# A two-layer encoder: the first two units behind each inner norm multiply x times gain, and the root and shift enter afterwards

## The chip, the core and the metric

The kernel runs on one core of a Trainium2 chip. The time is device microseconds of one execution from launch to end; a verdict compares medians of runs on the same chip. TensorE does the products, VectorE and ScalarE the elementwise work, POOL (GpSimd) and SP mostly issue loads.

## The reference, cut to what matters

Two sequences, 256 and 512 rows of 1024 features, go through two layers. Each layer normalizes, mixes, adds, normalizes again and applies a gated feed-forward:

```
def rmsnorm(x, g):  y = x * rsqrt(mean(x*x) + EPS);  return y * g
def modulate(h, shift, scale): return h * (1 + scale) + shift
h = modulate(rmsnorm(x, norm1_g), sh1, sc1);  x = x + g1 * mixer(h)
h = modulate(rmsnorm(x, norm2_g), sh2, sc2);  x = x + g2 * ((silu(h @ Wg) * (h @ Wu)) @ Wdown)
```

With r the reciprocal root of a row, w = g * (1 + scale) and s the shift, h = (x * w) * r + s. So h @ W = ((x * w) @ W) * r + s @ W: the root scales the result of a row, and the shift adds one vector per sequence. After the second layer a last norm gives the output. The mixer is attention and gated linear attention in layer 0 (even) and an mLSTM in layer 1 (odd).

## The kernel before, in words

All of x is kept turned: 8 tiles of 128 features (partitions) by 768 columns, 256 of the first sequence and 512 of the second. A product keeps fp32 precision by splitting both operands in two (hi and lo, float32r) and adding hi*hi, hi*lo and lo*hi: three products, each of 256 and 512 moving columns. A **feature unit** is 128 output features, k = 8 such triples for the projections from h (6 or 8 for the down projections, 4 for outb0 and outa0). A **token unit** is 256 output features with h as the stationary operand. plan_units (L69) lists the units in their order: bqk0, lowrank0, bv0, aq0, ak0, bg0, av0, outb0, outa0; then three groups gu00, down00, gu01, down01, gu02, down02; the odd layer's cq1, gates1, ck1, cv1 and co1, out1, then gu10 to down12. The gu units alternate gate (even n) and up (odd n).

Each engine has its own queue, written out in that order; semaphores tie them. Weights lie in four slots: SP's load of a unit waits for the products of the unit four before it (L594); ScalarE makes w_hi (split_to, L1213, L1221), VectorE w_lo (L1588, L1601), each one or two units ahead, in front of the work for the current unit. A feature unit's result lies in a pair of PSUM banks (L271); u.pair (L402) turns over three pairs in gu and down units and over two elsewhere, and a unit waits (wait_free, L738) until the former user of its pair has been read.

**Norms.** n = 0 is the one at the start, 1 stands behind outa0, 2 behind down02, 3 behind out1, 4 at the end. While the eight units before a norm give the last parts of x (residual, L1727; x is updated at L1737, 256 and then 512 columns), ScalarE squares each tile (squares_of and square_tile, L1274 to L1287) and VectorE sums the squares (add_squares, L1662). TensorE then adds over features with products of one column (norm_sums: L773 for the sum of seven, L776 for the last square), VectorE and ScalarE make mean, root and reciprocal (mean_root, L1669; ScalarE's norm, L1289), VectorE writes the root into six diagonal matrices (L1683), and TensorE spreads them over all partitions into bank pair 2 (L785). Then h is made tile by tile in VectorE's norm (L1678) and ScalarE's norm: normed = x * w * r (scaled, L1688), h_hi = normed + shift (L1297), h_lo = (normed + shift) - h_hi (rest, L1695), with two buffers of normed. The order on VectorE is scaled(0), scaled(1), rest(0), scaled(2), rest(1) and so on. TensorE runs the first two units behind the norm together (two_feature_tiles, L831), product k of both as soon as h of tile k is there, and then single units (feature_tile, L814).

A gu pair is taken so (hidden, L1312 and L1745): ScalarE makes silu of the gate unit into silu_g (L1322), VectorE prod = silu_g * up (L1757), ScalarE act_hi (L1326), VectorE act_lo (L1760). In gu00 to down01 VectorE also computes the modulation of the later norms (modulate, L1604; lines L1617 and L1620) from loads that POOL issues (L709), and TensorE sums it (L765). Those parts stand in VectorE's queue in front of the take of their unit (run, L1640).

## Time and profile before

| | us |
|---|---|
| median of 3 runs | 2128.09 (2118.55 to 2129.23) |
| profiled execution, its own time | 2124.51 |
| its span, first to last instruction | 2122.4 |
| TensorE busy with products | 2017.7 |
| VectorE busy | 992.6 |
| ScalarE busy | 601.7 |
| mean granted TensorE clock | 0.967 of full |

Some 2.1 us of the profiled execution's time lie around its span. Busy times are sums over the span; a granted clock of 1.00 is 2.4 GHz, 0.50 is 1.2 GHz. A time in a timeline is counted from the span's start.

### The profile page before, as it was taken

How to read it: one execution, taken by the hardware profiler on the slowest of the kernel's cores; microseconds unless marked ns; L12 is line 12 of the kernel's file. 1: busy time of each engine (PE TensorE's matmuls, PEld its weight loads, DVE VectorE, ACT ScalarE, POOL GpSimd, SP SyncE). 2: the span in 40 equal slices, each digit the busy share in tenths (PEclk: the TensorE clock that was granted, in tenths of full speed). 3: DMA queues.
4: the chain of work that ended last, by engine and by line, in shares of the span. 5: the costliest groups of instructions: out<-in, count | busy, mean ns of one | idle time of the engine just before them, and what ended most of it. 6: DMA issues, size and time to landing. Idle time of an engine off the chain costs nothing.

```text
span 2122.4 us, 28746 instructions
## 1 busy us (share of the span) xinstructions
PE 2017.7 (95%) x12081; PEld 1742.5 (82%) x12081; DVE 992.6 (47%) x1875; ACT 601.7 (28%) x1101; POOL 74.3 (4%) x121
## 2 busy tenths in 40 slices
PE   7879999988899999999998999998989999999998
PEld 2768888767788888888887788888878888888887
DVE  1877425684766665652235334544452222222224
ACT  3235224652321112211223333334232211211213
POOL 2010000000011101100000000000000000000000
PEclk9889999999899999999998999999989999999999
DMA  7343112012344444432223201021212222222212
GB/s 282 120 150 108 41 41 80 21 31 60 99 142 138 136 122 139 142 96 60 65 62 104 60 20 41 21 99 49 61 50 60 60 70 60 64 66 60 62 56 82
DMA packets 210249, 174.16 MB, mean 82 GB/s; under 512 B 10320, under 2 KB 196792, under 8 KB 208584
## 3 DMA queue, kind: packets, MB, share of 16 engines
q1 hardware_dynamic: 197536, 117.67, 18.5%
q0 software_dynamic: 12288, 48.35, 7.1%
q10 hardware_dynamic: 296, 6.29, 0.7%
q8 instruction: 96, 1.57, 0.3%
q14 instruction: 33, 0.27, 0.0%
HBM read 162.85 MB, written 9.44 MB: 81 GB/s over the span
## 4 chain that ended last, share of the span: by engine, by line
PE 87%; DVE 6%; ACT 4%; issue 2%; DMA 1%; POOL 0%; ACTq 0%; DVEq 0%; POOLq 0%
PE bank L824 60%; PE bank L790 9%; PE bank L842 4%; PE bank L1096 2%; PE bank L747 1%; PE bank L765 1%; DMA early_raw<-in_w_mod_dram 1%; ACT w_hi L1221 1%; DVE early_acc L1620 1%; DVE w_lo L1601 1%; PE bank L1018 1%; PE bank L908 1%; PE bank L1041 1%; PE bank L966 1%; PE bank L1068 1%
## 5 line engine op out<-in xcount | busy, mean ns | idle before, releaser
L824 PE MATMUL bank<-h_hi,w_hi 128*128 128x256 f32 x1600 | 409.4, 338 | 0.1
L824 PE MATMUL bank<-h_lo,w_hi 128*128 128x256 f32 x1600 | 407.5, 336 | 0.0
L824 PE MATMUL bank<-h_hi,w_lo 128*128 128x256 f32 x1600 | 407.3, 336 | 0.0
L1601 DVE TENSOR_TENSOR w_lo<-raw,w_hi 128x1024 fp32r<-128x1024 f32 (+4 forms) x195 | 239.0, 1230 | 340.2 <-ACT w_hi L1221 340.1
L824 PEld LDWEIGHTS bank<-h_hi,w_lo 128*128 128x128 f32 x1600 | 301.3, 188 | 33.6
L824 PEld LDWEIGHTS bank<-h_lo,w_hi 128*128 128x128 f32 x1600 | 301.4, 188 | 33.2
L824 PEld LDWEIGHTS bank<-h_hi,w_hi 128*128 128x128 f32 x1600 | 299.4, 188 | 34.2 <-issue 1.9
L1221 ACT ACTIVATE w_hi<-raw 128x1024 fp32r<-128x1024 f32 (+4 forms) x196 | 205.6, 1053 | 226.3 <-DMA raw<-in_ffn_w_down_dram 129.1
L790 PE MATMUL bank<-w_hi,h_hi 128*128 128x256 f32 x672 | 214.8, 320 | 18.1 <-DVE w_lo L1601 17.7
L790 PE MATMUL bank<-w_lo,h_hi 128*128 128x256 f32 x672 | 195.8, 291 | 0.0
L790 PE MATMUL bank<-w_hi,h_lo 128*128 128x256 f32 x672 | 195.6, 291 | 0.0
L1737 DVE SCALAR_TENSOR_TENSOR x<-bank,mod,x 128x256 f32<-128x256 f32 (+1 forms) x144 | 82.3, 613 | 229.6 <-PE bank L824 225.6
L824 PE MATMUL bank<-act_hi,w_hi 128*128 128x256 f32 x704 | 179.4, 337 | 4.6 <-issue 4.6
L824 PE MATMUL bank<-act_lo,w_hi 128*128 128x256 f32 x704 | 178.8, 336 | 0.0
L824 PE MATMUL bank<-act_hi,w_lo 128*128 128x256 f32 x704 | 178.7, 336 | 0.0
L790 PEld LDWEIGHTS bank<-w_hi,h_hi 128*128 128x128 f32 x672 | 134.5, 200 | 31.0 <-DVE w_lo L1601 18.1
L824 PEld LDWEIGHTS bank<-act_hi,w_hi 128*128 128x128 f32 x704 | 131.7, 188 | 19.8 <-issue 5.8
L824 PEld LDWEIGHTS bank<-act_lo,w_hi 128*128 128x128 f32 x704 | 132.4, 188 | 14.5
L824 PEld LDWEIGHTS bank<-act_hi,w_lo 128*128 128x128 f32 x704 | 132.4, 188 | 14.4
L790 PEld LDWEIGHTS bank<-w_lo,h_hi 128*128 128x128 f32 x672 | 134.6, 200 | 4.9 <-issue 3.8
L790 PEld LDWEIGHTS bank<-w_hi,h_lo 128*128 128x128 f32 x672 | 134.4, 200 | 0.0
L1620 DVE SCALAR_TENSOR_TENSOR late_acc<-late_raw,c_cols,late_acc 128x512 f32<-128x512 f32 x196 | 133.7, 746 | 0.6 <-DMA late_raw<-in_w_mod_dram 0.6
(274 smaller groups left out, 2251.7 us busy)
## 6 DMA issues: line engine op xcount, KB each, us to landing
raw<-in_ffn_w_gu_dram SPq DMA_DIRECT2D x176, 256.0 KB, 3.3
late_raw<-in_w_mod_dram POOLq DMA_DIRECT2D x56, 512.0 KB, 4.3
raw<-in_ffn_w_down_dram SPq DMA_DIRECT2D x64, 256.0 KB, 3.3
early_raw<-in_w_mod_dram POOLq DMA_DIRECT2D x24, 512.0 KB, 4.4
wide<-in_w_mod_dram SPq DMA_DIRECT2D x8, 1024.0 KB, 18.7
raw<-in_odd_w_in_dram SPq DMA_DIRECT2D x16, 512.0 KB, 4.4
raw<-in_even_w_in_dram SPq DMA_DIRECT2D x24, 256.0 KB, 5.0
x_kept<-x ACTq DMA_DIRECT2D x2, 3072.0 KB, 10.3
```

The costliest lines, as they stand in the source:

```text
L747: last = mm(bank[4 + c][0:2, :], c_cols[:, k, :], wide[k][:, c * 512:(c + 1) * 512], start=(k == 0), stop=(k == KD - 1))
L765: last = mm(mod_column(l, c0 // P + m)[:, s:s + 1], mod_acc(b)[:, s, m * P:(m + 1) * P], ones[:, 0:1], start=True, stop=True)
L790: last = mm(out, stationary[a], moving[b], start=(k == 0 and n == 0), stop=(k == K - 1 and n == 2))
L824: last = mm(pair(u.pair)[s], wk[a], seq(operand(o, k), s), start=(k == 0 and n == 0), stop=(k == u.ks - 1 and n == 2))
L842: last = mm(pair(u.pair)[s], wk[a], seq(operand(o, k), s), start=(k == 0 and n == 0), stop=(k == u.ks - 1 and n == 2))
L908: last = transpose(out[s][:, c:c + P], source(t), ident[:])
L966: last = mm(bank[6][:, d * P:(d + 1) * P], k_e[c][rows, t * P:(t + 1) * P], q_e[c][rows, t * P:(t + 1) * P], start=True, stop=True)
L1096: last = mm(bank[7][:, 0:C_V + 1], weights[d][:, c:c + P], z_cv[:, h, i, :], start=(i == froms[0]), stop=(i == froms[-1]))
L1221: fn(hi, r, ACT.Copy).then_inc(hi_ready, 1)
L1601: v.tensor_tensor(lo, r, hi.bitcast(F32), ALU.subtract).then_inc(unit_split, 1)
L1620: ins = v.scalar_tensor_tensor(acc, mod_raw(m)[:, kk, :], c, acc, ALU.mult, ALU.add)
L1737: last = v.scalar_tensor_tensor(seq(x[:, f, :], s), pair(u.pair)[s], mod[l][:, gate + f, s:s + 1], seq(x[:, f, :], s), ALU.mult, ALU.add)
```

## The change

The rows of h get two columns in front (hs_hi, hs_lo: 770 columns instead of 768), for the shift of the two sequences; a row so begins 8 bytes later in a step of 3080 bytes instead of 3072. All users of h read the rows at their new place.

At norms 1, 2 and 3 every residual unit is followed by plain (VectorE: normed = x * w, then h_lo = normed - h_hi) with ScalarE's copy into h_hi between. The first of them also writes the shift into the two columns. TensorE runs the first two units on these plain rows (two_plain_tiles); the first sequence's product has 258 moving columns, so that shift @ W comes out as two more result columns. The mean products stand behind k = 1 and the row products behind k = 3 of these two units. norm_sums is cut into norm_means and norm_rows for that, with no other change. ScalarE copies the spread root from bank pair 2 to SBUF (rstd_wide); scaled reads it there. After its fifth normed VectorE takes the first unit (take_first: the two shift columns, then result * root), after its sixth h_hi ScalarE applies shift and Identity or Silu (first_shifted); the second unit is taken at its usual place. h with root and shift is then made as before, over the plain rows, and serves from the third unit on, which waits for each of its tiles. VectorE and ScalarE split the weights of the third and fourth unit inside the norm. The cq units turn over three bank pairs.

The diff, without the declaration of the new semaphores and the cutting of norm_sums, with its indentation reduced:

```diff
@@ -134,9 +134,10 @@
-H = region(2 * KD * ROW)
-h_hi = at("h_hi", H, [P, KD, T], F32R)
-h_lo = at("h_lo", H + KD * ROW, [P, KD, T], F32R)
+H = region(2 * KD * (ROW + 8))
+hs_hi = at("hs_hi", H, [P, KD, 2 + T], F32R)
+hs_lo = at("hs_lo", H + KD * (ROW + 8), [P, KD, 2 + T], F32R)
+h_hi, h_lo = hs_hi[:, :, 2:2 + T], hs_lo[:, :, 2:2 + T]
@@ -150,6 +151,8 @@
 normed = [at(f"normed{b}", Z + 76 * KB + b * ROW, [P, T]) for b in range(2)]
+rstd_wide = at("rstd_wide", Z + 82 * KB, [P, T])
+first_bias = at("first_bias", Z + 85 * KB, [P, 2, 2])
@@ -271,6 +274,15 @@
     return bank[2 * g][:, 0:256], bank[2 * g + 1][:, 0:512]
+def wide_pair(g):
+    return bank[2 * g][:, 0:258], bank[2 * g + 1][:, 0:512]
+def wide_seq(ap, s):
+    return ap[:, 0:258] if s == 0 else ap[:, 258:770]
+NORM_AT = {1: (0, 1), 2: (1, 0), 3: (1, 1)}
@@ -399,7 +419,7 @@
         by = "act"
-    pairs = 3 if base in ("gu", "down") else 2
+    pairs = 3 if base in ("gu", "down", "cq") else 2
@@ -424,6 +444,7 @@
+MEANS_AFTER, ROWS_AFTER = 1, 3
@@ -473,6 +494,12 @@
     splittable.setdefault(-1 if u.prior is None else u.prior, []).append(u)
+def first_units(n):
+    return phase[{1: "gu00", 2: "cq1", 3: "gu10"}[n]][:2]
+FIRST_SCALED = {1: 1, 2: 2, 3: 4}
@@ -845,6 +879,29 @@
+    def two_plain_tiles(us, n):
+        for u in us:
+            pe.wait_ge(unit_split, u.i + 1)
+            wait_free(u)
+        pe.wait_ge(shift_ready, n)
+        for k in range(KD):
+            pe.wait_ge(plain_ready, KD * (n - 1) + k + 1)
+            for u in us:
+                wk = [slot_of(wt, u)[:, k * P:(k + 1) * P] for wt in (w_hi, w_lo)]
+                for m, (a, o) in enumerate(((0, 0), (0, 1), (1, 0))):
+                    for s in range(2):
+                        last = mm(wide_pair(u.pair)[s], wk[a], wide_seq((hs_hi, hs_lo)[o][:, k, :], s),
+                                  start=(k == 0 and m == 0), stop=(k == KD - 1 and m == 2))
+                if k == KD - 1:
+                    last.then_inc(group_full, 1)
+            if k < KD - 1:
+                last.then_inc(plain_read, 1)
+            if k == MEANS_AFTER:
+                norm_means(n)
+            if k == ROWS_AFTER:
+                norm_rows(n)
@@ -855,8 +912,19 @@
-    def feature_units(name, before=None, operand=normal, mix=None):
+    def feature_units(name, before=None, operand=normal, mix=None, norm=None):
         us = phase[name]
+        if norm:
+            two_plain_tiles(us[:2], norm)
+            after(us[0])
+            after(us[1])
+            pe.wait_ge(rstd_taken, norm)
+            feature_tile(us[2], operand, after_norm(norm), mix)
+            after(us[2])
+            for u in us[3:]:
+                feature_tile(u, operand, None, mix)
+                after(u)
+            return
@@ -1166,20 +1234,17 @@
     feature_units("outa0", lambda k: pe.wait_ge(mix_lo, B_HEADS + k + 1), turned(0), mix)
-    norm_sums(1)
     for g in range(FG):
-        feature_units(f"gu0{g}", after_norm(1) if g == 0 else None)
+        feature_units(f"gu0{g}", norm=1 if g == 0 else None)
         down_units(0, g)
-    norm_sums(2)
     mix = mix_odd()
-    feature_units("cq1", after_norm(2))
+    feature_units("cq1", norm=2)
...
     feature_units("out1", lambda k: pe.wait_ge(mix_lo, KD + k + 1), turned_odd, mix)
-    norm_sums(3)
     for g in range(FG):
-        feature_units(f"gu1{g}", after_norm(3) if g == 0 else None)
+        feature_units(f"gu1{g}", norm=3 if g == 0 else None)
@@ -1249,6 +1314,10 @@
         def take(u):
+            if u.name == "cq1" and u.n < 2:
+                if u.n == 1:
+                    first_shifted(2, u)
+                return
@@ -1282,21 +1351,52 @@
                 fn(dummy[:], ones[:, 0:1], ACT.Sqrt)
+            if n in NORM_AT and u.n == 0:
+                l, i = NORM_AT[n]
+                act.wait_ge(mod_ready, 7 if l == 0 else 1 + len(MOD_BLOCKS))
+                fn(hs_hi[:, :, 0:2], mod[l][:, (SH1, SH2)[i]:(SH1, SH2)[i] + KD, :], ACT.Copy).then_inc(shift_hi, 1)
...
             square_tile(n, u.n)
+            if n in NORM_AT:
+                act.wait_ge(plain_scaled, KD * (n - 1) + u.n + 1)
+                fn(h_hi[:, u.n, :], normed[u.n % 2][:], ACT.Copy).then_inc(plain_hi, 1)
...
+    def first_shifted(n, u):
+        act.wait_ge(first_scaled, FIRST_SCALED[n] + u.n)
+        dest, f = (z_o[:, 2 * u.n, :], ACT.Identity) if n == 2 else (silu_g[:], ACT.Silu)
+        for s in range(2):
+            last = fn(seq(dest, s), seq(dest, s), f, bias=first_bias[:, u.n, s:s + 1])
+        last.then_inc(free_act if n == 2 else silu_ready, 1)
     def norm(n, i):
+        if n in NORM_AT:
+            split_to(first_units(n)[0].i - 2)
...
         fn(mean_sq[:], mean_sq[:], ACT.Sqrt).then_inc(root_ready, 1)
+        if n in NORM_AT:
+            split_to(first_units(n)[0].i - 1)
...
             return
+        if n in NORM_AT:
+            act.wait_ge(rstd_full, TILES * (n + 1))
+            for s in range(2):
+                last = fn(seq(rstd_wide, s), pair(2)[s], ACT.Copy)
+            last.then_inc(rstd_taken, 1)
...
             act.wait_ge(normed_ready, KD * n + f + 1)
+            if n in NORM_AT:
+                if f < KD - 1:
+                    act.wait_ge(plain_read, (KD - 1) * (n - 1) + f + 1)
+                else:
+                    act.wait_ge(group_full, first_units(n)[1].g1)
...
             last.then_inc(h_hi_ready, 1)
+            if n in NORM_AT and f == 5:
+                first_shifted(n, first_units(n)[0])
@@ -1314,6 +1414,8 @@
             j = u.n // 2
+            if g == 0 and u.n == 0:
+                return
@@ -1681,12 +1783,19 @@
             v.tensor_scalar(rstd_diag[:, t, :], ident[:], mean_sq[:, t:t + 1], None, ALU.mult).then_inc(rdiag_ready, 1)
+        if n in NORM_AT:
+            split_to(first_units(n)[0].i - 1)
         dve.wait_ge(rstd_full, TILES * (n + 1))
+        rows = pair(2)
+        if n in NORM_AT:
+            dve.wait_ge(rstd_taken, n)
+            rows = seq(rstd_wide, 0), seq(rstd_wide, 1)
...
                 m = v.scalar_tensor_tensor(seq(normed[f % 2], s), seq(x[:, f, :], s), gain[l][i][:, f, s:s + 1],
-                                           pair(2)[s], ALU.mult, ALU.mult)
+                                           rows[s], ALU.mult, ALU.mult)
@@ -1703,6 +1812,8 @@
                 rest(f - 1)
+            if n in NORM_AT and f == 4:
+                take_first(n, first_units(n)[0])
@@ -1723,6 +1834,49 @@
         m.then_inc(mix_lo, 1)
+    def plain(n, f, u):
+        l, i = NORM_AT[n]
+        if f == 0:
+            dve.wait_ge(shift_hi, n)
+            v.tensor_tensor(hs_lo[:, :, 0:2], mod[l][:, (SH1, SH2)[i]:(SH1, SH2)[i] + KD, :],
+                            hs_hi[:, :, 0:2].bitcast(F32), ALU.subtract).then_inc(shift_ready, 1)
+        dve.wait_ge(free_dve, u.free[0][1])
+        if f >= 2:
+            dve.wait_ge(plain_ready, KD * (n - 1) + f - 1)
+        for s in range(2):
+            last = v.tensor_scalar(seq(normed[f % 2], s), seq(x[:, f, :], s), gain[l][i][:, f, s:s + 1], None, ALU.mult)
+        last.then_inc(plain_scaled, 1)
+        dve.wait_ge(plain_scaled, KD * (n - 1) + f + 1)
+        dve.wait_ge(plain_hi, KD * (n - 1) + f + 1)
+        v.tensor_tensor(h_lo[:, f, :], normed[f % 2][:], h_hi[:, f, :].bitcast(F32), ALU.subtract).then_inc(plain_ready, 1)
+    def take_first(n, u):
+        dve.wait_ge(group_full, u.g1)
+        v.tensor_copy(first_bias[:, u.n, :], wide_pair(u.pair)[0][:, 0:2])
+        if n == 2:
+            dest = z_o[:, 2 * u.n, :]
+        else:
+            dest = (silu_g, prod)[u.n][:]
+            if n == 3:
+                dve.wait_ge(act_ready, FT)
+        sums = wide_pair(u.pair)[0][:, 2:258], wide_pair(u.pair)[1]
+        for s in range(2):
+            last = v.tensor_tensor(seq(dest, s), sums[s], seq(rstd_wide, s), ALU.mult)
+        if n == 2 or u.n == 0:
+            last.then_inc(first_scaled, 1)
+            return
+        link(last)
+        a0 = 0 if n == 1 else FT
+        dve.wait_ge(silu_ready, a0 + 1)
+        for s in range(2):
+            last = v.scalar_tensor_tensor(seq(prod, s), seq(prod, s), first_bias[:, 1, s:s + 1], seq(silu_g, s),
+                                          ALU.add, ALU.mult)
+        last.then_inc(free_dve, 1)
+        dve.wait_ge(act_hi_ready, a0 + 1)
+        v.tensor_tensor(act_lo[:, 0, :], prod[:], act_hi[:, 0, :].bitcast(F32), ALU.subtract).then_inc(act_ready, 1)
@@ -1737,6 +1891,8 @@
             last.then_inc(free_dve, 1)
+            if n in NORM_AT:
+                plain(n, f, u)
@@ -1746,6 +1902,10 @@
         def take(u):
+            if g == 0 and u.n < 2:
+                if u.n == 1:
+                    take_first(2 * l + 1, u)
+                return
@@ -2084,7 +2244,8 @@
     mix = mix_odd()
-    run(phase["cq1"] + phase["gates1"])
+    run(phase["cq1"][:2], lambda u: take_first(2, u) if u.n == 1 else None)
+    run(phase["cq1"][2:] + phase["gates1"])
```

## Rows read from the trace of the kernel before

**Rows 1.** The page: busy us of each engine (share of the span) xinstructions.
```profile
PE 2017.7 (95%) x12081; PEld 1742.5 (82%) x12081; DVE 992.6 (47%) x1875; ACT 601.7 (28%) x1101; POOL 74.3 (4%) x121
```

**Rows 2.** Chain of waits: start us, us, what; products resuming behind norms 1, 2, 3.
```profile
563.86 24.96 PE bank L824 x144
...
1155.48 17.20 PE bank L824 x96
...
1570.77 116.48 PE bank L824 x672
```

**Rows 3.** Timeline at norm 3: start us, us, engine, line, operation, count, [idle before].
```profile
1539.67 1.39 PE L773 MATMUL bank<-ones,square_sum 128*128 128x1 f32 x12
...
1539.87 1.14 DVE L1737 SCALAR_TENSOR_TENSOR x<-bank,mod,x 128x256 f32<-128x256 f32 x2 [3.38 <-PE bank L824]
...
1541.94 1.50 PE L776 MATMUL bank<-ones,square 128*128 128x1 f32 x12 [0.88 <-ACT square L1278]
...
1544.68 2.93 PE L785 MATMUL bank<-rstd_diag,ones 128*128 128x128 f32 x12 [1.24 <-DVE rstd_diag L1683]
1547.64 2.19 DVE L1688 SCALAR_TENSOR_TENSOR normed<-x,gain,bank 128x256 f32<-128x256 f32 x4 [2.04 <-PE bank L785]
...
1549.97 1.15 DVE L1695 SCALAR_TENSOR_TENSOR h_lo<-normed,mod,h_hi 128x256 fp32r<-128x256 f32 x2
...
1563.38 2.43 DVE L1695 SCALAR_TENSOR_TENSOR h_lo<-normed,mod,h_hi 128x256 fp32r<-128x256 f32 x4
```

**Rows 4.** Windows behind norm 1: stretch, PE busy, granted clock, DMA share, GB/s.
```profile
544.00:546.00 2.00, 1.61 (x5) 0.50 0.00 0
550.00:552.00 2.00, 2.00 (x13) 0.99 0.00 0
```

**Rows 5.** Timeline of VectorE: the last update of x before norm 2.
```profile
1124.28 1.14 DVE L1737 SCALAR_TENSOR_TENSOR x<-bank,mod,x 128x256 f32<-128x256 f32 x2 [1.14 <-PE bank L824]
```

**Rows 6.** Timeline of ScalarE behind norm 1: table load and first Silu.
```profile
558.71 1.28 ACT L1322 ACT_TABLE_LOAD   x1
562.86 0.87 ACT L1322 ACTIVATE silu_g<-bank 128x256 f32<-128x256 f32 x2 [2.86 <-PE bank L842]
```

**Rows 7.** Timeline of VectorE in the first gate and up units: modulation, then prod.
```profile
565.85 0.88 DVE L1617 TENSOR_SCALAR late_acc<-late_raw,c_cols 128x512 f32<-128x512 f32 x2
...
570.62 1.01 DVE L1757 TENSOR_TENSOR prod<-silu_g,bank 128x256 f32<-128x256 f32 x2
```

**Rows 8.** Timeline of VectorE in outa0, the units before norm 1.
```profile
502.22 1.14 DVE L1737 SCALAR_TENSOR_TENSOR x<-bank,mod,x 128x256 f32<-128x256 f32 x2 [1.41 <-PE bank L842]
...
512.02 0.69 DVE L1601 TENSOR_TENSOR w_lo<-raw,w_hi 128x512 fp32r<-128x512 f32 x1 [1.43 <-ACT w_hi L1221]
...
513.50 1.14 DVE L1737 SCALAR_TENSOR_TENSOR x<-bank,mod,x 128x256 f32<-128x256 f32 x2
...
526.77 1.14 DVE L1737 SCALAR_TENSOR_TENSOR x<-bank,mod,x 128x256 f32<-128x256 f32 x2
529.76 1.23 DVE L1601 TENSOR_TENSOR w_lo<-raw,w_hi 128x1024 fp32r<-128x1024 f32 x1 [1.86 <-ACT w_hi L1221]
...
531.78 1.14 DVE L1737 SCALAR_TENSOR_TENSOR x<-bank,mod,x 128x256 f32<-128x256 f32 x2
```

**Rows 9.** Timeline of ScalarE in the seventh unit of outa0.
```profile
527.94 0.85 ACT L1278 ACTIVATE square<-x 128x768 f32<-128x768 f32 x1 [3.21 <-DVE x L1737]
528.69 1.04 ACT L1221 ACTIVATE w_hi<-raw 128x1024 fp32r<-128x1024 f32 x1
```

**Rows 10.** Instructions on tile y: duration ns min/median/max, first and last start.
```profile
L1742 DVE TENSOR_SCALAR y<-x,v_cols x8: 619/620/622, 2063.6 to 2107.3; 128x768 f32<-128x768 f32 x8
```

**Rows 11.** Timeline of TensorE in the odd mixer.
```profile
1330.27 1.90 PE L1096 MATMUL bank<-z_cv,weights 128*128 128x257 f32 x8
...
1336.26 0.92 PE L1096 MATMUL bank<-z_cv,weights 128*128 128x257 f32 x3 [2.66 <-DVE h_o L1999]
```

**Rows 12.** Window around the stall of rows 11, columns as in rows 4.
```profile
1334.00:1338.00 4.00, 1.74 (x9) 1.00 0.00 0
```

More of the change, by code:

```diff
@@ L313, in build @@
         h_ready = sem("h_ready")
+        shift_hi = sem("shift_hi")
+        shift_ready = sem("shift_ready")
+        plain_scaled = sem("plain_scaled")
+        plain_hi = sem("plain_hi")
+        plain_ready = sem("plain_ready")
+        plain_read = sem("plain_read")
+        rstd_taken = sem("rstd_taken")
+        first_scaled = sem("first_scaled")
         silu_ready = sem("silu_ready")
@@ L769, in norm_sums, with norm_means @@
             def norm_sums(n):
+                norm_means(n)
+                if n != 4:
+                    norm_rows(n)
+            def norm_means(n):
                 pe.wait_ge(sq_summed, (KD - 2) * (n + 1))
@@ L778, in norm_sums, with norm_rows @@
                 last.then_inc(mean_full, 1)
-                if n == 4:
-                    return
+            def norm_rows(n):
                 for t in range(TILES):
@@ L846, in two_feature_tiles @@
                     mix_steps(us[0], k, mix)
+            def two_plain_tiles(us, n):
[16 more added lines that the diff above has]
+                    if k == MEANS_AFTER:
+                        norm_means(n)
+                    if k == ROWS_AFTER:
+                        norm_rows(n)
             def after(u):
```

## The prediction

> **What bounds it now.** I read the page's busy table first: TensorE is busy 95% of the span [rows 1], so what can be won is where it stands still. The chain of waits then shows, behind each inner norm, two units of products that begin late, and where plain products resume: 563.86, 1155.48 and 1570.77 us [rows 2]. A unit of eight products takes 24.96/3 = 8.32 us there, so 1.04 us per unit and product; the third unit of each group ends at 572.2, 1163.8 and 1579.1 us. Those three ends are what I compare with, since from there on TensorE runs as it does now.
>
> The timeline of norm 3 [rows 3] says what the hole is made of. The last product ends about 1539.7, x's last update runs 1539.87 to 1541.0, the two batches of mean products (1.39 and 1.50 us) end by 1543.4, the twelve row records (2.93 us) at 1547.6, and then VectorE makes h: two rows of normed, the first h_lo done at 1551.1 (3.5 us after the start D), each further one 2.24 us later, the eighth at 1565.8, 18.15 us after D. TensorE restarts at the first h_lo and is at 1.2 GHz for its first 5.3 us or so (in norm 1 granted clock 0.50 at its restart and 0.99 in the stretch from 550 us [rows 4]), 2.65 us lost, which is already in the three ends above. The reader should see that h's production is a chain of VectorE and ScalarE as long as the two units' 16.6 us.
>
> **The change, part by part, behind norms 2 and 3.** TensorE no longer waits for the root: it runs the first two units on x times gain. It waits for x's last update, because a first unit's bank pair is that of the last one: S = 1124.28 + 1.17 = 1125.45 [rows 5] and 1541.05. Products 0 and 1 of both units take 4.16 us, the mean products 2.9: M = S + 7.05. VectorE's mean, root and diagonals stand beside products 2 and 3 (4.16 us): with the row records they take 4.2 us in all now (1543.4 to 1547.6). Then the row records: at least half of their 2.93 us at 1.2 GHz, at most all; I take 1.5, the clock being full. ScalarE copies them to SBUF, a new step on the path, 0.87 us by the copy of the same shape in silu_g [rows 6]. So D = M + 4.16 + 1.5 + 0.9 + handovers = M + 6.6. VectorE's two w_lo (1.2 us each) fit between diagonals and D.
>
> The full chain of h is still to come: 18.15 us. Two things are put into it. After the fifth normed, VectorE takes the first unit: two products from PSUM of the shape of prod's 1.01 us [rows 7], and a two-column copy, 1.1 us together. After the sixth h_hi, ScalarE shifts that unit: in norm 2 some 1.1 us of Identity, which fits its 1.1 us of slack; in norms 1 and 3 a table load of 1.28 [rows 6] and a Silu of 1.1, 2.4 against 1.1, so 1.35 more. The eighth h is ready at M + 25.85 (norm 2) or M + 27.2.
>
> TensorE has finished both first units by M + 4.16 + 1.5 + 8.32 = M + 14.0, and the third unit then eats h faster (1.04) than it comes (2.24). It ends one product after the eighth h: M + 26.9 or M + 28.25. Norm 2: 1132.5 + 26.9 = 1159.4 against 1163.8, **4.4 us won**. Norm 3: 1548.1 + 28.25 = 1576.35 against 1579.1, **2.75 won**. Most of the 13 us hole is thus not filled but moved into the third unit.
>
> That table load is the row's 1.28 us. The Trainium skill ("ScalarE: Activation LUTs", the rules for kernel authors) budgets about 2.7 us for every switch of set, which would put 1.4 us more into norms 1 and 3, 2.8 in all, and speaks against putting a Silu amid the Identities.
>
> **Behind norm 1** the units before are short: half as many products, 4.2 us each. VectorE's cycle per unit is already 5.01 us at the end (x starts at 526.77 and 531.78 [rows 8]): x 1.17, ScalarE's square 0.75 to its next instruction, w_hi 1.07 [rows 9], then w_lo and the square sum, 2.02. The change adds per unit VectorE's scaling (0.6 to 0.75: y's same operation on 768 columns takes 0.62 [rows 10], in two pieces I take 0.75), ScalarE's copy for h_hi (0.75 on, like the square) and VectorE's h_lo (0.95). The scaling hides beside the square; copy and h_lo do not, and h_lo is hidden behind w_hi only where w_hi is 1024 columns. Full units: 5.01 + 0.75 = 5.8. Half ones: 1.17 + 0.75 + 0.85 + 0.87 to the end of h_lo, 3.65, and 1.48 from w_lo to the next x (512.02 to 513.50): 5.15. From 502.22: 4.4 (no square sum yet; the 16-element shift rest is in it), four of 5.15, two of 5.8: the last x starts at 538.8, not 531.78, **7 us late**. No other queue is late: SP's loads wait for TensorE's groups, POOL issues its two loads at the end of the group.
>
> TensorE, idle from about 532.8, begins at S = 540.0, with its clock down: 2.65 us more, M = 549.7, third unit ends 578.0. One more wait appears: behind the eighth h VectorE has two parts of modulation (565.85 to 570.62, 4.8 us [rows 7]) before it takes the second unit (1.1 + 1.2), ScalarE's act_hi (0.9) follows, and only then w_hi and w_lo of the fifth unit (1.05 + 1.2): M + 37.4, wanted at M + 28.25 + 8.32 = 36.6. So 0.85: norm 1 **costs 578.0 + 0.85 - 572.2 = 6.65 us**.
>
> **What costs nothing.** Two more columns on 48 moving operands a norm: 48 x 2/2.4 GHz = 0.04 us. The same scaling in norms 2 and 3: cycle 5.8 under a unit's 6.24 and 8.5 us; the cover in norm 2 is only 0.4 us, and an operation longer by more would pay eight times.
>
> **Sum.** -4.4 - 2.75 + 6.65 = -0.5 us on the profiled 2124.5 us. Open is the clock in the third unit: from M + 18 on TensorE waits some 1.2 us behind each product. Against a fall speaks that a single stall of 2.66 us [rows 11] left the clock at 1.00 [rows 12]; for it, that after the hole it is down each time, and that here four such gaps follow each other. A fall costs nothing while h is late (2.08 a product at half clock is under 2.24), then at most 2.65 us after the third unit. Bounds 0 and 3 x 2.65 = 8; I take one fall, 2.65. The sum is then +2 on either footing. The profiled run lies 3.6 under the median of three, 2128.09, whose spread is 2118.55 to 2129.23; I forecast against the median: **2130**.
>
> The Trainium skill ("TensorE: Matmul & The Clock Gate", HAM oscillation) warns of loops whose repeated idle gaps throttle TensorE again each time; by that rule all three third units would lose the 2.65, and the time would be 2135.6. The trace bears it out for the holes behind the norms, not for a stall of this size.
>
> **Rivals.** (a) *The holes close.* The third unit also streams on, as if h were there: per norm 1.2 + 16.6 + 2.9 + 1.5 + 8.3 = 30.5 us after the last product, against 39.4 now in norms 2 and 3, 9 us each, and norm 1 about as much: 2128 - 27 = 2101. It needs the eighth h 5 to 6 us sooner than 18.15 us of measured VectorE work allow, and x's last update unmoved. 8%, a milder form included in which only norm 1's backlog stays away (2128 - 12 = 2116). (b) *Rows of h off their old boundary.* Each row of h now begins 8 bytes on, with a step of 3080 bytes, for all products, 108 feature units (900 us) and the token units too, not only for the first two. If a pair of 345 ns lost 4.2 ns by it (1.2%), the kernel would be 10.6 us slower; at 3%, 27 us, 2157. Nothing shows it: products that stream 257 columns from rows of z_cv with an odd step took 1.55 us for eight records, under 0.2 each [rows 11], no slower than 257 columns need. But for weights loaded from such rows, as the token units do, there is no row. 8%. (c) *Clock and backlog at their upper ends*: row records at 2.93 instead of 1.5 (+4.3), three falls (+8), norm 1's cycle 0.3 longer in eight units (+2.4): 2128 - 0.5 + 14.7 = 2142. 7%. (d) *It does not do what it says*: the plain products of norms 2 and 3 also wait, for example for the second first-unit's weights. Those are split before the last x, so no; it would be 7 slower, inside the forecast's bounds. 1%.
>
> **Numbers.** A measurement here tells about 0.5% (10.6 us) from no change. The forecast (a small gain at two norms, a loss at the first) has 76%, of which 2 are runs that scatter out below: 2119 to 2138 by its open terms and half of the runs' spread. The range reaches a little towards (a) below and (c) above: 2118 to 2140. Faster by over 0.5%: (a) and those 2, 10%. Slower: (b) 8 and most of (c), 6, 14%. Within: 74 + 1 + 1 = 76%.
>
> **What would show it.** In the new trace: the last x before norm 1 starts near 539, with TensorE idle before it; first plain products at about 540, 1125.4 and 1541 us plus what went before; in each third unit four products on end and then gaps of 1 to 2 us waiting for h_lo; a table load between two h_hi; the clock at or after the third unit. I am wrong if the third units run without waits, if the cycle before norm 1 stays at 5.0 us, or if products far from the norms have changed from 345 ns a pair.

## The result and the profile after

The changed kernel takes 2141.06 us, median of 5 runs (2134.79 to 2143.58), beside 2122.4 us of the kernel before, median of 5: ratio 1.0075, 95% interval [1.0046, 1.0104]. (The ratios here come from all executions of both kernels; the quotient of the two medians alone would be 1.0088.) A second measurement on another chip gave 1.0081 [1.0063, 1.0099]. So it is slower by three quarters of a per cent, 1 us above my range of 2118 to 2140. The profiled execution took 2136.84 us beside 2124.51 before, with 12.6 us more span.

The page of the changed kernel, span and busy times (share of the span) of the engines:

```profile
span 2135.0 us, 28946 instructions
PE 2021.5 (95%) x12081; PEld 1736.3 (81%) x12081; DVE 1037.9 (49%) x1968; ACT 624.2 (29%) x1134; POOL 74.3 (3%) x121
```

Beside [rows 1]: VectorE's 45 us more are the scaling, the second h_lo and the taking of the first units, as costed. TensorE is busy 3.8 us longer, although its mean granted clock is higher, 0.976 against 0.967. That is the first hint of where the loss lies.

**Norm 1.** VectorE before norm 1, then the start D of h's chain and the w_lo of the fifth unit:

```profile
499.51 1.14 DVE L1891 SCALAR_TENSOR_TENSOR x<-bank,mod,x 128x256 f32<-128x256 f32 x2 [1.62 <-PE bank L876]
...
514.39 1.14 DVE L1891 SCALAR_TENSOR_TENSOR x<-bank,mod,x 128x256 f32<-128x256 f32 x2
...
519.64 1.14 DVE L1891 SCALAR_TENSOR_TENSOR x<-bank,mod,x 128x256 f32<-128x256 f32 x2
...
524.89 1.14 DVE L1891 SCALAR_TENSOR_TENSOR x<-bank,mod,x 128x256 f32<-128x256 f32 x2
...
530.69 1.13 DVE L1891 SCALAR_TENSOR_TENSOR x<-bank,mod,x 128x256 f32<-128x256 f32 x2
...
536.71 1.14 DVE L1891 SCALAR_TENSOR_TENSOR x<-bank,mod,x 128x256 f32<-128x256 f32 x2
...
554.08 2.21 DVE L1797 SCALAR_TENSOR_TENSOR normed<-x,gain,rstd_wide 128x256 f32<-128x256 f32 x4 [2.29 <-ACT rstd_wide L1385]
...
582.07 1.23 DVE L1703 TENSOR_TENSOR w_lo<-raw,w_hi 128x1024 fp32r<-128x1024 f32 x1
```

The cycle is now 5.25 us in half units, where I had 5.15, and 5.80 and 6.02 in the two full ones, where I had 5.8. Before it was 5.01 in the last full unit [rows 8] and 4.05 in half ones, from the row below to the one at 513.50 in [rows 8]:

```profile
509.45 1.14 DVE L1737 SCALAR_TENSOR_TENSOR x<-bank,mod,x 128x256 f32<-128x256 f32 x2
```

TensorE in the same stretch of the changed kernel:

```profile
537.94 0.98 PE L894 MATMUL bank<-hs_hi,w_hi 128*128 128x258 f32 x2 [7.33 <-DVE x L1891]
567.47 0.62 PE L858 MATMUL bank<-hs_hi,w_hi 128*128 128x256 f32 x2 [1.77 <-DVE hs_lo L1804]
569.71 0.61 PE L858 MATMUL bank<-hs_hi,w_hi 128*128 128x256 f32 x2 [0.93 <-DVE hs_lo L1804]
572.19 0.62 PE L858 MATMUL bank<-hs_hi,w_hi 128*128 128x256 f32 x2 [1.17 <-DVE hs_lo L1804]
583.35 0.61 PE L858 MATMUL bank<-hs_hi,w_hi 128*128 128x256 f32 x2 [0.33 <-DVE w_lo L1703]
```

7.33 us idle before the plain products, gaps of 0.9 to 1.8 us in the third unit, and the wait for the fifth unit's w_lo: the schedule is the one forecast. From x's first update to the fifth unit it is 583.35 - 499.51 = 83.84 us; before, 563.86 + 16.64 - 502.22 = 78.28 [rows 2, 8]. Norm 1 costs 5.6 us.

**Norms 2 and 3.** Windows of the changed kernel: the third unit behind norm 1, then the products behind the mean products of norms 2 and 3 (columns: stretch, length, busy us and count of PE, PEld, DVE, ACT, POOL, granted clock, DMA share, GB/s):

```profile
564.00:574.00 10.00, 6.14 (x32) 4.67 (x31) 9.78 (x21) 5.98 (x10) 0.00 (x0) 1.00 0.14 41
1145.00:1147.00 2.00, 2.00 (x8) 1.72 (x8) 2.00 (x3) 0.00 (x0) 0.00 (x0) 0.50 0.03 8
1557.00:1560.00 3.00, 3.00 (x12) 2.50 (x11) 3.00 (x7) 0.32 (x1) 0.00 (x0) 0.50 0.00 0
```

In this execution the gaps of the third unit do not bring the clock down: TensorE is busy 6.14 of 10 us there and has 1.00. It falls to 1.2 GHz elsewhere, in the plain products about 1 us behind the mean products, for about 3.3 us in norms 2 and 3. That is not so in every execution. In the profile of `changed_again`, the same kernel (below), the third unit behind norm 3 also loses its clock, from a gap of 1.75 us on:

```profile
1576.33 0.91 PE L858 MATMUL bank<-hs_hi,w_hi 128*128 128x256 f32 x2 [1.75 <-DVE hs_lo L1804]
```

```profile
1577.00:1579.00 2.00, 1.95 (x7) 1.30 (x6) 1.97 (x5) 1.99 (x4) 0.00 (x0) 0.50 0.00 0
```

All profiles of kernels with the new order taken together, the clock fell in 9 of the 14 third units behind norms 2 and 3 and in none of the five behind norm 1; in the plain products of norms 2 and 3 it fell 8 times in 14. By the rule that the Trainium skill gives ("TensorE: Matmul & The Clock Gate", HAM oscillation), whose example has longer gaps than these, repeated idle gaps throttle TensorE again each time; at gaps of 0.9 to 1.8 us these traces agree in some executions and not in others.

**Far from the norms.** The chain of waits of the changed kernel, stretches in which nothing was rebuilt; first gate and up units of layer 0, later the last groups of layer 1:

```profile
593.70 25.42 PE bank L858 x144
...
838.88 33.88 PE bank L858 x192
...
1188.56 33.83 PE bank L858 x192
...
1899.47 219.64 PE bank L858 x1248
```

The same pieces in the kernel before, whose [rows 2] end where these begin:

```profile
590.50 25.07 PE bank L824 x144
...
832.67 33.40 PE bank L824 x192
...
1181.15 33.93 PE bank L824 x192
...
1889.49 216.58 PE bank L824 x1248
```

144 matmuls, 25.07 us before and 25.42 now; 1248 of them 216.58 and 219.64, 1.4% more. And the last rows hold something that I had passed over: two pieces of 192 matmuls of the same kind took 33.40 and 33.93 us in one and the same execution before. One step (a unit with one tile of h or act: three pairs of 256 and 512 columns, six matmuls) takes 1.040 us at one pace (116.48/112 in [rows 2]) and 1.060 at the other (33.93/32). A piece behind other work has about 0.1 us more at its start, so that 24 steps at 1.040 are the 25.07 above. In the changed kernel a step takes 1.053 us with act and 1.055 to 1.056 with h. So against the slow pace the changed kernel even gains a little (33.83 against 33.93). The theories were: **A**, the row layout slows products everywhere; **B**, only the move by 128 bytes of what lies behind h does; **C**, the new order of work does.

### The profile page after: what moved, and what is told of

It reads as the page before. It is cut to its first block, busy times and chain, and to the rows that moved or that the text cites. A ratio compares the mean times of both kernels' runs of the same rounds, so it can differ in the third digit from the quotient of the medians.

```text
span 2135.0 us, 28946 instructions
## 1 busy us (share of the span) xinstructions
PE 2021.5 (95%) x12081; PEld 1736.3 (81%) x12081; DVE 1037.9 (49%) x1968; ACT 624.2 (29%) x1134; POOL 74.3 (3%) x121
## 4 chain that ended last, share of the span: by engine, by line
PE 83%; DVE 8%; ACT 4%; issue 2%; DMA 2%; POOL 0%; ACTq 0%; DVEq 0%; SPq 0%; POOLq 0%
PE bank L858 59%; PE bank L824 9%; PE bank L1164 2%; PE bank L894 1%; PE bank L774 1%; PE bank L792 1%; DVE hs_lo L1804 1%; DVE normed L1797 1%; PE bank L876 1%; DVE early_acc L1722 1%; DMA early_raw<-in_w_mod_dram 1%; DVE w_lo L1703 1%; PE bank L1086 1%; PE bank L1109 1%; ACT w_hi L1286 1%
## 5 line engine op out<-in xcount | busy, mean ns | idle before, releaser
L858 PE MATMUL bank<-hs_hi,w_hi 128*128 128x256 f32 x1600 | 414.9, 341 | 11.7 <-DVE hs_lo L1804 11.3
L858 PE MATMUL bank<-hs_lo,w_hi 128*128 128x256 f32 x1600 | 411.7, 339 | 0.0
L858 PE MATMUL bank<-hs_hi,w_lo 128*128 128x256 f32 x1600 | 411.4, 338 | 0.0
L858 PEld LDWEIGHTS bank<-hs_hi,w_hi 128*128 128x128 f32 x1600 | 299.9, 189 | 50.6 <-DVE hs_lo L1804 14.4
L858 PEld LDWEIGHTS bank<-hs_hi,w_lo 128*128 128x128 f32 x1600 | 302.5, 189 | 35.8
L858 PEld LDWEIGHTS bank<-hs_lo,w_hi 128*128 128x128 f32 x1600 | 302.5, 189 | 34.9
L824 PE MATMUL bank<-w_hi,hs_hi 128*128 128x256 f32 x672 | 212.4, 316 | 18.1 <-DVE w_lo L1703 17.7
L824 PE MATMUL bank<-w_lo,hs_hi 128*128 128x256 f32 x672 | 193.3, 288 | 0.0
L824 PE MATMUL bank<-w_hi,hs_lo 128*128 128x256 f32 x672 | 192.5, 287 | 0.0
L824 PEld LDWEIGHTS bank<-w_hi,hs_hi 128*128 128x128 f32 x672 | 131.7, 196 | 30.8 <-DVE w_lo L1703 18.1
L1428 ACT ACTIVATE act_hi<-prod 128x768 fp32r<-128x768 f32 x44 | 37.2, 846 | 341.2 <-DVE prod L1917 329.5
```

What stands on the lines that cost most here:

```text
L824: last = mm(out, stationary[a], moving[b], start=(k == 0 and n == 0), stop=(k == K - 1 and n == 2))
L858: last = mm(pair(u.pair)[s], wk[a], seq(operand(o, k), s), start=(k == 0 and n == 0), stop=(k == u.ks - 1 and n == 2))
L1428: fn(act_hi[:, j, :], prod[:], ACT.Copy).then_inc(act_hi_ready, 1)
```

## The experiments

**The layout taken alone, and what lies behind it.** `layout_only` is the kernel before with two columns ahead of each row of h:

```diff
-        H = region(2 * KD * ROW)
-        h_hi = at("h_hi", H, [P, KD, T], F32R)
-        h_lo = at("h_lo", H + KD * ROW, [P, KD, T], F32R)
+        PAD = 2
+        H = region(2 * KD * (ROW + 4 * PAD))
+        hs_hi = at("hs_hi", H, [P, KD, PAD + T], F32R)
+        hs_lo = at("hs_lo", H + KD * (ROW + 4 * PAD), [P, KD, PAD + T], F32R)
+        h_hi, h_lo = hs_hi[:, :, PAD:PAD + T], hs_lo[:, :, PAD:PAD + T]
```

> The kernel before with nothing of the change but the row layout: two unused columns ahead of each row of h, so rows start 8 bytes on, step 3080 bytes, and what lies behind H moves by 128 bytes. Theory A (the layout makes products slower everywhere): the down units' x updates come 6.32 us apart instead of 6.24, and the time is 12 to 16 us over before, ratio 1.006 to 1.0075. Theory B (only the 128-byte move of what lies behind H matters): 6.32 us in the down units, but h's own units as before, +4 to +8 us. Theory C (the new order of work, not the layout): 6.24 us and the time of before within 3 us.

Measured: 1.0049 [1.0026, 1.0071], and 1.0048 [1.0032, 1.0063] on another chip (`layout_only_again`, below). Its chain of waits has the changed kernel's pieces to 0.01 us:

```profile
588.97 25.42 PE bank L826 x144
...
834.16 33.88 PE bank L826 x192
...
1895.47 219.63 PE bank L826 x1248
```

The pace goes with the layout, and C falls as the cause of it; the price is 10 us, not the 12 to 16 expected, so two thirds of the loss.

`base_moved` leaves h alone and moves only what lies behind it:

```diff
-        H = region(2 * KD * ROW)
+        H = region(2 * KD * ROW + 128)
```

> The kernel before with 128 unused bytes behind h and nothing else: h's rows as they were, act, turned, odd and all else behind H 128 bytes on. Theory A (8-byte start or 3080-byte step of h's rows): time and 6.24 us as before. Theory B (the move): the down units' x updates 6.32 us apart, +4 to +8 us in all. Theory C: as before.

Measured: 1.0021 [1.0000, 1.0042]. Its chain, a stretch of h's units, one of act's, and one of h's again:

```profile
591.97 25.54 PE bank L824 x144
...
702.20 25.39 PE bank L824 x144
...
1188.41 33.41 PE bank L824 x192
```

Act's products go at 1.053 (25.39), as in the changed kernel, though no operand of them changed but its place. So the move of 128 bytes slows act's products by itself, which the prediction had not seen; in the whole time the interval just touches 1.000. And h's rows, which did not move at all, ran at 1.060 here (25.54) where they ran at 1.040 before, and at 1.040 where they had 1.060 (33.41 against 33.93). That is not the layout: unmoved operands take either pace, and in no trace did it change while the products of one operand ran on without a break.

`h_8_bytes_only` is the other half: `layout_only` with 128 bytes more behind h, so that all behind it moves by 256.

> The kernel before with h's rows 8 bytes on (step 3080 bytes) but what lies behind H moved by 256 bytes, so that act, turned and odd keep their residue. Theory D: down units at their old paces (8.32 or 8.48 us in groups of 8 tiles), h's units at 8.42 to 8.43; the time between before and layout_only, ratio 1.002 to 1.004. If the 8 bytes do nothing and only the move of 128 bytes counts: 1.000. If h's 8 bytes are all of it: 1.005.

Measured: 1.0028 [1.0013, 1.0044]; h's units 25.43, act's first group 25.07, within the forecast. The parts add, as far as intervals of 0.15 to 0.2% on two chips can tell: 0.28% for h's 8 bytes, 0.21% for the 128-byte move, 0.48% together.

`act_steps` moves act by another distance in each of its six groups.

```diff
-        Z = region(90 * KB)
+        Z0 = region(90 * KB + 512)
+        Z = Z0 + 512
...
-        act_hi = at("act_hi", Z, [P, GT, T], F32R)
-        act_lo = at("act_lo", Z + GT * ROW, [P, GT, T], F32R)
+        STEP = {(0, 0): 32, (0, 1): 64, (0, 2): 96, (1, 0): 128, (1, 1): 192, (1, 2): 256}
+        acts = {lg: [at(f"act_{o}{d}", Z0 + d + b * GT * ROW, [P, GT, T], F32R) for b, o in enumerate(("hi", "lo"))]
+                for lg, d in STEP.items()}
```

(The diff leaves out the places that read and write act.)

> The kernel before with act moved by another number of bytes in each of its six groups of down units: 32, 64, 96, 128, 192 and 256, all else behind H 512 bytes on. Three products of a unit with a tile, six matmuls, took 1.040 or 1.060 us in unmoved tiles and 1.053 with act 128 bytes on. Theory D: 1.053 at 128, 1.040 or 1.060 at 256, something else (up to 1.053) between; if only multiples of 128 count, 32 to 96 stay at 1.040 or 1.060. Rival (not the place, but chance at each restart): 1.040 and 1.060 in all six.

Measured: 1.0057 [1.0038, 1.0077] in the whole. By group: at 32 bytes 25.07 us a piece of 144, the pace 1.040; at 64 bytes 25.23, so 1.047. The updates of x show the others, in groups of 6 tiles (96 bytes; 256 bytes) and of 8 (128; 192):

```profile
1095.59 1.14 DVE L1738 SCALAR_TENSOR_TENSOR x<-bank,mod,x 128x256 f32<-128x256 f32 x2 [1.69 <-PE bank L825]
1101.89 1.14 DVE L1738 SCALAR_TENSOR_TENSOR x<-bank,mod,x 128x256 f32<-128x256 f32 x2 [1.69 <-PE bank L825]
...
1710.30 1.14 DVE L1738 SCALAR_TENSOR_TENSOR x<-bank,mod,x 128x256 f32<-128x256 f32 x2 [6.15 <-PE bank L825]
1718.73 1.14 DVE L1738 SCALAR_TENSOR_TENSOR x<-bank,mod,x 128x256 f32<-128x256 f32 x2 [6.16 <-PE bank L825]
...
1912.39 1.14 DVE L1738 SCALAR_TENSOR_TENSOR x<-bank,mod,x 128x256 f32<-128x256 f32 x2 [6.21 <-PE bank L825]
1920.87 1.14 DVE L1738 SCALAR_TENSOR_TENSOR x<-bank,mod,x 128x256 f32<-128x256 f32 x2 [6.20 <-PE bank L825]
...
2082.00 1.14 DVE L1738 SCALAR_TENSOR_TENSOR x<-bank,mod,x 128x256 f32<-128x256 f32 x2 [1.75 <-PE bank L825]
2088.36 1.14 DVE L1738 SCALAR_TENSOR_TENSOR x<-bank,mod,x 128x256 f32<-128x256 f32 x2 [1.74 <-PE bank L825]
```

6.30/6 = 1.050 at 96, 8.43/8 = 1.054 at 128, 8.48/8 = 1.060 at 192, 6.36/6 = 1.060 at 256. So 128 gives 1.053 again, 256 is a pace of the unmoved tiles, and 64 and 96 lie between: the pace does depend on the place, in steps finer than 128 bytes. Whether the 1.040 at 32 and the 1.060 at 192 are a matter of the place or one of the two paces, one execution does not tell.

**The changed kernel without the layout's cost.** `rows_aligned` pads rows to start on 32 bytes (776 columns, all behind h 512 bytes on); `rows_256` pads them to 832 columns, so that rows and all behind them move by multiples of 256 bytes:

```diff
-        H = region(2 * KD * (ROW + 8))
-        hs_hi = at("hs_hi", H, [P, KD, 2 + T], F32R)
-        hs_lo = at("hs_lo", H + KD * (ROW + 8), [P, KD, 2 + T], F32R)
-        h_hi, h_lo = hs_hi[:, :, 2:2 + T], hs_lo[:, :, 2:2 + T]
+        PAD = 64
+        H = region(2 * KD * (ROW + 4 * PAD))
+        hp_hi = at("hp_hi", H, [P, KD, PAD + T], F32R)
+        hp_lo = at("hp_lo", H + KD * (ROW + 4 * PAD), [P, KD, PAD + T], F32R)
+        hs_hi, hs_lo = hp_hi[:, :, PAD - 2:], hp_lo[:, :, PAD - 2:]
+        h_hi, h_lo = hp_hi[:, :, PAD:PAD + T], hp_lo[:, :, PAD:PAD + T]
```

(This is `rows_256`; `rows_aligned` has PAD = 8.)

> The changed kernel with rows padded to 776 columns, h from column 8 and the shift in columns 6 and 7: rows of h start on 32 bytes again, step 3104 bytes; what lies behind H moves by 512 bytes instead of 128. Theory A: the 12 to 14 us of slower products go, about 2127, ratio to before 1.000 to 1.003, pieces of 144 products 25.07 us instead of 25.42. Theory B: as the changed kernel (2141) if any move does it, 2127 if it was the 128. Theory C: 2141, ratio 1.007.

Measured: 1.0036 [1.0018, 1.0055]. Theory A as I had put it, a matter of a row's start on 32 bytes, is wrong: h's pieces take 25.33 us, better than 25.42, but not 25.07. With a step of 3104 bytes the eight rows of h_hi lie 32, 64 and so on to 256 bytes off their old places, so this pace is a mean over eight places.

> The changed kernel with rows of 832 columns, h from column 64, shift in columns 62 and 63: each row of h, and all behind H (moved by 4096 bytes), keeps its old residue of 256 bytes. Theory D (products slow down where operands leave their old residue of 256 bytes: act, turned and odd by the 128-byte move, h by its 8 bytes): down units in the stretches of 8 tiles come 8.32 or 8.48 us apart as in the kernels with the old residue, never 8.42, and the time is 5 to 8 us under the changed kernel. Rival (any moved or padded layout has it): 8.42 us, 2141 or ratio 1.007.

Measured: 0.9997 [0.9979, 1.0015], 2123.80 us beside 2142.22 of the changed kernel on the same chip. Its chain:

```profile
594.98 25.07 PE bank L860 x144
...
954.67 178.19 PE bank L860 x1008
...
1890.92 216.58 PE bank L860 x1248
```

25.07 and 216.58 as before; the middle row is the 1.060 pace (before 174.85 for as many, changed 177.37). Theory D had put the time 5 to 8 us under the changed kernel; it is 18 under. The whole loss of the changed kernel goes with 62 columns of padding, more than `layout_only` puts on. Not all of that is shown in the traces: the two profiled executions lie 10.2 us apart (spans 2134.1 and 2123.9), the medians 18.4. `changed_again` is the changed kernel on that chip:

> The changed kernel as it is, beside the others on one chip. Against norms 2 and 3 alone (2129.2 against 2125.8 before, on the last chip) it should show what norm 1 costs in full: by the trace 5.5 us, so ratio to before 1.0015 to 1.004; by the two ratios so far (1.0075 and 1.0010) 13 us, ratio about 1.007.

It gave 1.0081, the second of the two forecasts.

**The norms apart.** In `norms_2_and_3` norm 1 keeps its old order, in the layout of the change (the diff leaves out the semaphore counts, which now begin with norm 2):

```diff
-        NORM_AT = {1: (0, 1), 2: (1, 0), 3: (1, 1)}
+        NORM_AT = {2: (1, 0), 3: (1, 1)}
...
+            norm_sums(1)
             for g in range(FG):
-                feature_units(f"gu0{g}", norm=1 if g == 0 else None)
+                feature_units(f"gu0{g}", after_norm(1) if g == 0 else None)
```

> The changed kernel with norm 1 in its old order (no plain products, x's cycle before norm 1 back at 5.0 us), norms 2 and 3 changed, layout as changed. By the trace norm 1 loses 5.5 us net, so 2141 - 5.5 = 2135.5, ratio to before 1.005. Rival: norm 1's loss is only an offset that later waits would swallow, 2141 and 1.0075. All theories on the layout leave this the same.

Measured: 1.0010 [0.9990, 1.0030], 2129.20 us, on the chip where `layout_only` had 2135.83. The forecast of 1.005 missed: without norm 1's new order the kernel is 0.65% faster than the changed one, not 0.26%. The two norms win 0.39% on the layout that they share, where I read some 4.5 us, 0.2%, from the trace; with intervals of 0.2% on each ratio the two may still agree.

`norms_2_3_rows_256` puts both remedies together, and `norm_1_rows_256` is its complement, norm 1 alone in the new order.

> As rows_256, but norm 1 in its old order: the norms that win, without the layout's cost. Theory D: 4.5 us (the two norms, by the trace) under the kernel before, ratio 0.998, interval about 0.002 to each side. If the layout is not the cause: as norms_2_and_3, 1.001.

Measured: 0.9967 [0.9950, 0.9984], 2117.12 us.

> Only norm 1 in the new order, norms 2 and 3 as before, rows of 832 columns (residues of 256 bytes kept). If the terms add: norm 1 costs 6.2 us (2123.8 of rows_256 less 2117.1 of norms_2_3_rows_256 is 6.7 by medians; 6.65 forecast), ratio to before 1.003. If norm 1's loss is hidden or made good in later stretches: 1.000. If it also brings what the changed kernel lost beyond the layout: 1.006.

Measured: 1.0033 [1.0017, 1.0049]: norm 1 costs 7 us of its own.

> Norms 2 and 3 in the new order with rows of 832 columns once more: 0.9967 again, interval under 1.000, so that it beats both kernels on a second measurement. If 0.9967 was chance, 1.000.

Measured: 1.0001 [0.9983, 1.0019]. The gain did not come back, and the two intervals share no more than 0.9983 to 0.9984. The two profiles of this one kernel show of what such a difference is made. First execution:

```profile
589.79 25.08 PE bank L861 x144
...
1882.31 216.58 PE bank L861 x1248
```

second execution, the same instructions:

```profile
591.93 25.54 PE bank L861 x144
...
1890.42 220.73 PE bank L861 x1248
```

4.15 us in the last piece alone, by the pace that the piece happened to have. The spans were 2115.3 and 2128.6 us; 4.8 of the 13.3 us between them lie in the mixer of layer 1, of which more below. So the mean, 0.9984, is my best figure, and that this version beats the kernel before is not shown; that it beats the changed one is.

> The row layout alone once more, beside h's part alone: 1.005 again (interval then 1.0026 to 1.0071), every stretch of its profile within 1 us of the last, since products at 1.053 us per three pairs do not depend on how TensorE restarts. If it comes to 1.008 here, the layout is all of the changed kernel's loss and the last chip's figure was low.

Measured: 1.0048. The expectation on its profile failed in one place: the products agree to 0.1 us a piece, but the mixer of layer 1 took 189.6 us from its first to its last product with weights, not 186.2. Windows of `layout_only`, then of `layout_only_again`, in that mixer:

```profile
1320.00:1350.00 30.00, 27.32 (x174) 24.35 (x173) 16.50 (x43) 9.84 (x27) 0.00 (x0) 0.94 0.04 14
1380.00:1410.00 30.00, 28.26 (x195) 25.58 (x194) 20.10 (x60) 12.24 (x34) 0.00 (x0) 1.00 0.11 36
```

```profile
1320.00:1350.00 30.00, 27.31 (x184) 24.56 (x183) 16.07 (x43) 10.54 (x30) 0.00 (x0) 1.00 0.04 11
1380.00:1410.00 30.00, 28.25 (x180) 25.70 (x178) 17.51 (x51) 11.39 (x30) 0.00 (x0) 0.89 0.12 36
1431.00:1434.00 3.00, 3.00 (x9) 2.35 (x7) 0.00 (x0) 0.41 (x3) 0.00 (x0) 0.50 0.28 117
```

The granted clock (the third figure from the end) falls at different places in the two: 0.06 x 30 = 1.8 us in the first, 0.11 x 30 = 3.3 us in the second, and there 1.7 us more by the fall around 1431. That makes up the 3.4 us between the two, to 0.2. This is a second source of scatter: over all profiles the mixer took from 184.7 us, without a fall, to 190.1.

## Why the prediction was right or wrong

**The sum was right, the case was not.** My terms for the three norms gave -0.5 us, and with one fall of the clock +2. With the layout's cost taken out, the changed kernel measures 0.9997 (`rows_256`): -0.6 us, +-4. That is partly luck: by the trace the three norms come to 5.6 - 2.7 - 2.0 = +0.9 us, since what norm 1 cost less made good a part of what norms 2 and 3 won less, and an interval of +-4 us would have held any of these sums. Luck also has a part in how near 2141 lies to the range: I started from 2128.09, a median of three, and five executions of the kernel before gave 2122.4. The forecast failed in what it held to cost nothing. The change put every row of h on another place, and I looked for a price in the 48 moving operands behind each norm, 0.04 us. My own sign of being wrong came true: products far from the norms went from 347 ns a pair (1.040/3) to 351 or 352. Rival (b) named the mechanism, with 1.2% on a pair and 10.6 us; measured are 1.4% where the old pace was 1.040 (25.42 against 25.07), a gain of 0.3% where it was 1.060 (33.83 against 33.93), and 0.48% or 10 us in the whole. I gave it 8% because "nothing shows it", and argued against it from rows of z_cv with an odd step. Those rows do not bear that out: eight records take 1.90 us in [rows 11] (my 1.55 is from their first start to that of the next product), so 0.19 us each at the least, where 257 columns at the pace of a step (2304 columns in 1.040 us) would take 0.12. They could hide a loss of several per cent, while 1% on 900 us decides this case. A cost that touches every product must be bounded to 0.1%, or carry its chance. And I drew the rival too narrowly: it spoke of h's rows, but some 0.2 of the 0.48% came from act, turned and odd, which moved by 128 bytes because the region ahead of them grew.

**Term by term.** Norm 1: forecast +6.65, in the trace +5.6, timed alone 0.33% or 7 us. The last x was to start at 538.8 and did at 536.71, but the stage before began 2.7 us earlier; from first to last update 37.2 us, forecast 36.6. Right. Norm 2: forecast -4.4. From x's last update to the gates' unit it is 1180.11 - 1134.44 = 45.67 us after and 1172.67 - 1124.28 = 48.39 before, so -2.7. What is missing is 1.6 us of the half clock in the window 1145 to 1147: D came 8.18 us after the mean products (1151.22 - 1143.04), not 6.6. I had put one fall into a third unit; in this execution it came in the plain products, in two norms. In other executions it came in third units too, as said above, and there it cost little: in `changed_again` the gap before the seventh h shrank from 1.15 us to 0.58, as I had argued that a fall costs nothing while h is late. And the first product starts 1.51 us after x's update began, not 1.17: -4.4 + 1.6 + 0.35 = -2.45. Norm 3: forecast -2.75; from x's last update to the first down unit 148.30 us after, 148.53 before, of which the slower products explain 1.8 us (118.30 for 672 matmuls in `layout_only` against 116.48 before), so -2.0: again 1.65 for the clock, against it 1.35 for the table load, which I had charged and which cost nothing. Rows of ScalarE behind norm 1:

```profile
566.39 1.12 ACT L1395 ACTIVATE hs_hi<-normed,mod 128x256 fp32r<-128x256 f32 x2 [1.99 <-DVE normed L1797]
567.53 1.28 ACT L1370 ACT_TABLE_LOAD   x1
568.82 1.12 ACT L1370 ACTIVATE silu_g<-silu_g,first_bias 128x256 f32<-128x256 f32 x2
569.85 2.15 ACT L1395 ACTIVATE hs_hi<-normed,mod 128x256 fp32r<-128x256 f32 x4
```

The load and the Silu delay the seventh h_hi by 1.2 us, but VectorE takes the eighth normed in the meantime, and from D to the end of the eighth h_lo it is 19.1 us in norm 1 as in norm 2, where no table is loaded. The load is 1.28 us, as in [rows 6]; the Silu starts 1.29 us after the load does. The Trainium skill ("ScalarE: Activation LUTs", the rules for kernel authors) budgets about 2.7 us for a switch; this trace does not agree.

**What stays open.** The parts of the changed kernel, timed apart, add to 0.48 (layout) + 0.33 (norm 1) and for norms 2 and 3 between -0.39 (`norms_2_and_3` less `layout_only`) and 0.01 (`norms_2_3_rows_256_again`), mean of three -0.24: 0.57% together against 0.78% measured. The 0.2 left are within the intervals of the parts, each +-0.2, and I have no mechanism for them. Nor have I one for another difference: the layout costs 0.48% by itself, but 0.84% by `changed_again` less `rows_256`, on one chip. Why a place costs what it does is also open. The Trainium skill ("Advanced Engine Details and Errata", SBUF Cachelines) has lines of 16 bytes and full speed where accesses stay in one; read so, h's 8-byte start would be a cost and a start on 32 bytes none. The traces agree with the first alone: act moved by 128 bytes is slower, and rows on 32 bytes still took 25.33. What chooses between 1.040 and 1.060 was not tried. Nor was another place of the weights against h and act.

## What to carry to other kernels

An edit that pads or shifts an operand of every product is not local: compare the duration of untouched pieces far from the edit first, and time the layout by itself before the idea it serves. Here 62 unused columns, which keep all addresses at their old residue of 256 bytes, gave back what the change had lost; of smaller paddings only 8 columns were tried, which gave back about half. And where VectorE is the slower engine between two products, work added to its cycle is paid in full (norm 1), while the same work under longer units is free (norms 2 and 3): such a change should be made only where the unit before is long.

## What was unexpected of the hardware

- A step of three pairs of matmuls (256 and 512 columns, fp32r) takes 1.040 or 1.060 us with operands at their old place; a pace held for up to 1248 matmuls on end. The same kernel took 216.58 and 220.73 us for the same piece. With act 128 bytes on it is always 1.053, with h 8 bytes on 1.055 to 1.056 (118.30/112), in every execution profiled.
- Runs of the kernel before spread from 2114.03 to 2137.32 us on one chip, 1.1%, and two measurements of one kernel, of 11 and 12 runs, gave 0.9967 and 1.0001. In the two profiles of that kernel the pace and the clock in the mixer make up most of the difference; that they make the whole spread is not shown.
- The same third unit with gaps of 0.9 to 1.8 us kept its clock at 1.00 in one execution (TensorE busy 6.14 of 10 us) and fell to 0.50 in others. And the clock fell for 3.3 us behind the one-column mean products of norms 2 and 3, where TensorE had had no idle time since a gap of 1.5 us some 8 us earlier; behind the same products of norm 1 it stayed at 1.00.
